# Token sums of the first half mixed and stored in the last block of the first phase, and two down splits ahead of the last products

## The chip, the cores and the metric

The kernel runs on one core of one Trainium2 chip. The metric is the device time of one execution in microseconds, the median of several runs; lower is better. The engines are TensorE (PE in the profile, its weight loads PEld), VectorE (DVE), ScalarE (ACT), GpSimd (POOL) and SyncE (SP). SP and POOL start the DMA transfers here, each through a queue of its own.

## What is computed

One layer of a hybrid encoder over 2048 tokens of width 1024, all in float32:

```
h = RMSNorm(x);  p = h @ W_in
A = sliding-window attention(p);  B = HGRN2 gated recurrence(p)
x = x + concat(A, B) @ W_out
h = RMSNorm(x);  gate, up = h @ W_gate_up
x = x + (silu(gate) * up) @ W_down          # 2816 hidden columns
```

Each float32 operand of a product is split into a high part (rounded for the fast matmul format) and a low part (the rest), and a product is three matmuls: high by high, low by high, high by low (`three_passes`, L201 to L211). ACT makes a high part by a copy, DVE makes the low part by a subtraction.

## The kernel before

There are two phases, each a block of its own in the program: all engines meet at its end.

**Phase A** (`build_phase_a`) takes 4 blocks of 512 tokens. In a block PE runs 16 chunks of weights: 12 of W_in (named KV, QA0, ... Q23, I23, G23) and 4 of W_out (WO0 to WO3), each in up to 4 groups of 128 tokens (or 2 heads) of about 3 us. The list `STEPS`, made by `block_steps`, says which smaller step follows which group: splits of the next chunk (`split_hi` on ACT, `split_lo` on DVE), attention steps, and recurrence steps such as `hb` and `hc` (gates), `ds` (the running state on DVE, L1015 and L1019), `att`, `o` (outputs, PE L833 and L838) and `on1` to `on3` (their norm). Every engine walks the same list in order and does its own part of each step; `left_out` or `of_next_block` skips steps in the last block. SP loads chunk n into one of two stages `a_w_stage` as soon as DVE has split chunk n-2 (L397). In WO0 to WO3 DVE adds each product to the residual (L919), ACT squares it (L571), and POOL stores it to the DRAM tensor `x_mid`. The projection results go through two banks `a_pj`, so a group needs the group two before it to have been read. In the last block SP loads the first 2 x 128 tokens to be mixed (L415) and the norm weights `n2w` (L417) into the stages, when the last splits have left them.

**Phase B** (`build_ffn`) forms the gate and up products by a scheme with 7 products (`P1`, `P6`, `P5`, `P2`, `P7`, `P3`, `P4`) in place of 8, on sums and differences of quarters of the weights and of the tokens. For the tokens, a half of 1024 tokens is 4 pairs of 128-token tiles. `mix` on DVE scales a pair by `rs` (the reciprocal root of its mean square, made by POOL) and `n2w` (2 instructions of 1024 columns), then makes 4 sums or differences of 512 columns; POOL stores three pieces of each pair into the DRAM tensor `hc`. When all 4 pairs are stored, POOL loads the seven operands `hx` from `hc` into two buffers; PE transposes each (`turn`, L1349), ACT and DVE split it (`h_high`, `h_low`). Before the first unit, DVE's order is: pair 0, the mix and the first split of the first weights, pairs 1 to 3, the second weight split, the first operand. Then 44 units (2 halves x 22 column tiles) run; the second half's pairs are mixed at units 4, 7, 10 and 13.

At the end 88 **down steps** multiply the stored activations by W_down. A step's operands are split by `high_down` on ACT and `low_down` on DVE. SP's order there is: the loads of steps 0 and 1, the store of the last unit's activations (`store_a`), the residual load (`load_res`, 2 MB), the loads of step 2 and on. DVE's order is: low parts of step 0, `up_halves`, `a_products` of the last unit, low parts of step 1.

## Time and profile before

| What | us |
|---|---|
| Median of 3 runs (2302.03 to 2303.75) | 2302.94 |
| The profiled execution, its own time | 2303.67 |
| Span of its trace | 2301.9 |
| PE busy in the span | 2199.6 (96%) |
| DVE busy | 1261.1 (55%) |
| ACT busy | 928.7 (40%) |
| POOL busy | 143.9 (6%) |
| Mean granted clock of PE | 0.984 of full speed |

Phase A runs from 0 to about 885 us, the first 44 units of phase B to about 1811 us, the down steps from there to the end.

How to read it: 96% busy says that PE is the engine that sets the time nearly everywhere. The page also cuts the span in 40 slices of 57.5 us with the busy tenths of each engine; PE has 9 in nearly all of them, and 3 and 6 in the two slices at the change of phase, where the granted clock is lower as well (7 tenths and 7 tenths of full speed as the mean of each slice).

### The profile page before, as it was taken

What the parts mean: (1) busy time and instruction counts of PE and PEld (TensorE: products, weight loads), DVE (VectorE), ACT (ScalarE), POOL (GpSimd) and SP (SyncE); (2) the same over time, 40 slices, a digit from 0 to 9 for tenths busy, and PEclk for the clock granted to TensorE, in tenths of its full rate; (3) what the DMA queues carried; (4) which work ended last, traced back from release to release, by engine and by line L of the source; (5) the groups of instructions that cost most, each with busy time, mean ns of one, the idle gap of its engine ahead of it and who ended that gap; (6) DMA issues with size and microseconds to landing.
All of it is one profiled execution on the core that took longest, in us unless ns stands there. A gap on an engine that the chain in (4) does not pass through costs nothing.

```text
span 2301.9 us, 31427 instructions
## 1 busy us (share of the span) xinstructions
PE 2199.6 (96%) x12640; PEld 1903.9 (83%) x12640; DVE 1261.1 (55%) x1902; ACT 928.7 (40%) x1674; POOL 143.9 (6%) x154
## 2 busy tenths in 40 slices
PE   7999999999999993699999999999999999999999
PEld 7889988998898893588888888888888788888887
DVE  4675466447635754556666566555555334343333
ACT  4773386448535741333333333333333222232222
POOL 2001201010112002100000000000000000000000
PEclk9999999999999997799999999999999999999999
DMA  3412332323133125623334233222221435445453
GB/s 133 146 58 102 119 112 74 129 92 112 56 138 119 56 93 189 240 84 133 133 133 151 83 137 119 83 82 83 83 83 65 150 139 187 178 180 186 172 193 134
DMA packets 81648, 284.00 MB, mean 123 GB/s; under 512 B 8608, under 2 KB 17056, under 8 KB 66912
## 3 DMA queue, kind: packets, MB, share of 16 engines
q1 hardware_dynamic: 67296, 221.96, 27.2%
q0 software_dynamic: 14208, 60.04, 7.1%
q8 instruction: 100, 1.64, 0.3%
q14 instruction: 44, 0.36, 0.0%
HBM read 227.44 MB, written 54.53 MB: 122 GB/s over the span
## 4 chain that ended last, share of the span: by engine, by line
PE 58%; DMA 2%; DVE 1%; issue 0%; DVEq 0%; POOL 0%; ACT 0%; SPq 0%; POOLq 0%
PE b_bank_A L209 3%; PE b_bank_A L208 3%; PE b_bank_C L209 3%; PE b_bank_B L209 3%; PE b_bank_B L208 3%; PE b_bank_B L210 3%; PE b_bank_A L210 3%; PE b_bank_C L208 3%; PE b_bank_C L210 3%; PE b_hx_bank L1400 3%; PE b_hx_bank L1402 3%; PE b_hx_bank L1401 3%; PE b_bank_D L208 2%; PE b_bank_D L209 2%; PE b_bank_D L210 2%; PE b_hx_bank L1349 1%
## 5 line engine op out<-in xcount | busy, mean ns | idle before, releaser
L1418 DVE TENSOR_TENSOR b_dn_lo<-b_dn_stage,b_dn_hi 128x1024 fp32r<-128x1024 f32 x88 | 107.8, 1226 | 303.8 <-ACT b_dn_hi L1302 303.7
L208 PE MATMUL a_pj<-a_w_hi,a_hT_hi 128*128 128x256 f32 x896 | 259.0, 289 | 1.7 <-issue 1.7
L209 PE MATMUL a_pj<-a_w_lo,a_hT_hi 128*128 128x256 f32 x896 | 253.3, 283 | 0.0
L210 PE MATMUL a_pj<-a_w_hi,a_hT_lo 128*128 128x256 f32 x896 | 253.3, 283 | 0.0
L1302 ACT ACTIVATE b_dn_hi<-b_dn_stage 128x1024 fp32r<-128x1024 f32 x88 | 93.3, 1060 | 341.8 <-PE b_bank_D L1402 310.6
L208 PEld LDWEIGHTS a_pj<-a_w_hi,a_hT_hi 128*128 128x128 f32 x896 | 171.6, 191 | 6.8 <-issue 4.4
L855 DVE TENSOR_TENSOR a_w_lo<-a_w_stage,a_w_hi 128x2048 fp32r<-128x2048 f32 (+1 forms) x64 | 137.9, 2155 | 71.2 <-ACT a_w_hi L518 71.2
L209 PEld LDWEIGHTS a_pj<-a_w_lo,a_hT_hi 128*128 128x128 f32 x896 | 171.7, 192 | 0.0
L210 PEld LDWEIGHTS a_pj<-a_w_hi,a_hT_lo 128*128 128x128 f32 x896 | 171.6, 191 | 0.0
L1400 PE MATMUL b_hx_bank<-b_dn_hi,b_a_hi 128*128 128x512 f32 x352 | 138.3, 393 | 4.9 <-DVE b_a_lo L1418 4.8
L1402 PE MATMUL b_hx_bank<-b_dn_hi,b_a_lo 128*128 128x512 f32 x352 | 137.9, 392 | 0.0
L1401 PE MATMUL b_hx_bank<-b_dn_lo,b_a_hi 128*128 128x512 f32 x352 | 137.9, 392 | 0.0
L208 PE MATMUL b_bank_A<-b_h_hi_B,b_w_hi 128*128 128x512 f32 x352 | 137.6, 391 | 0.0
L208 PE MATMUL b_bank_B<-b_h_hi_T,b_w_hi 128*128 128x512 f32 x352 | 137.3, 390 | 0.0
L209 PE MATMUL b_bank_A<-b_h_lo_B,b_w_hi 128*128 128x512 f32 x352 | 137.2, 390 | 0.0
L210 PE MATMUL b_bank_A<-b_h_hi_B,b_w_lo 128*128 128x512 f32 x352 | 137.0, 389 | 0.0
L210 PE MATMUL b_bank_B<-b_h_hi_T,b_w_lo 128*128 128x512 f32 x352 | 137.0, 389 | 0.0
L209 PE MATMUL b_bank_B<-b_h_lo_T,b_w_hi 128*128 128x512 f32 x352 | 136.9, 389 | 0.0
L1335 ACT ACTIVATE b_gate<-b_u 128x512 f32<-128x512 f32 x44 | 27.8, 632 | 241.3 <-DVE b_u L1541 241.3
L518 ACT ACTIVATE a_w_hi<-a_w_stage 128x2048 fp32r<-128x2048 f32 (+1 forms) x64 | 115.3, 1801 | 1.5 <-DMA a_w_stage<-w_whole 1.5
L1418 DVE TENSOR_TENSOR b_w_lo<-b_mixed_w,b_w_hi 128x1024 fp32r<-128x1024 f32 x88 | 107.6, 1222 | 11.5 <-ACT b_w_hi L1277 11.5
L1321 ACT ACTIVATE b_s<-b_bank_C 128x512 f32<-128x512 f32 x44 | 26.4, 600 | 206.3 <-PE b_bank_C L210 206.3
(266 smaller groups left out, 5557.6 us busy)
## 6 DMA issues: line engine op xcount, KB each, us to landing
a_w_stage<-w_whole SPq DMA_DIRECT2D x56, 1024.0 KB, 4.7
b_gu_stage<-w_gu SPq DMA_DIRECT2D x44, 1024.0 KB, 5.2
b_dn_stage<-w_dn SPq DMA_DIRECT2D x88, 512.0 KB, 3.4
a_mid<-b_a SPq DMA_DIRECT2D x88, 256.0 KB, 4.1
b_a_stage<-a_mid SPq DMA_DIRECT2D x88, 256.0 KB, 3.6
b_hx<-hc POOLq DMA_DIRECT2D x14, 1024.0 KB, 5.1
a_x_res<-x_pad POOLq DMA_DIRECT2D x16, 512.0 KB, 4.4
x_mid<-a_x_res POOLq DMA_DIRECT2D x16, 512.0 KB, 3.4
```

The costliest lines, as they stand in the source:

```text
L208: pe.matmul(out, stationary[0](k), moving[0](k), start=(k == 0 and not adds), stop=False, skip_group_check=adds)
L209: pe.matmul(out, stationary[0](k), moving[1](k), start=False, stop=False, skip_group_check=adds)
L210: last = pe.matmul(out, stationary[1](k), moving[0](k), start=False, stop=(k == ends), skip_group_check=adds)
L518: act.activation(w_hi[s][:, :, 0:cols], w_stage[s][:, :, 0:cols], ACT.Copy).then_inc(w_hi_ready.sem, 1)
L855: dve.tensor_tensor(w_lo[s][:, :, 0:cols], w_stage[s][:, :, 0:cols], w_hi[s][:, :, 0:cols].bitcast(F32), ALU.subtract).then_inc(w_lo_ready ...
L1302: act.activation(f.dn_hi[b][:], f.dn_stage[b][:], ACT.Copy).then_inc(f.dn_hi_ready, 1)
L1321: act.activation(f.s5[:], f.bank["C"][:], ACT.Copy).then_inc(f.s5_ready, 1)
L1335: act.activation(f.gate[1][:], f.u2[:], ACT.Silu).then_inc(f.silu_ready[1], 1)
L1400: pe.matmul(f.down[i], f.a_hi[b][:, rows], f.dn_hi[b][:, cols], start=(j == 0), stop=False)
L1401: pe.matmul(f.down[i], f.a_hi[b][:, rows], f.dn_lo[b][:, cols], start=False, stop=False)
L1402: last = pe.matmul(f.down[i], f.a_lo[b][:, rows], f.dn_hi[b][:, cols], start=False, stop=(j == FT - 1))
L1418: dve.tensor_tensor(out, full, hi.bitcast(F32), ALU.subtract).then_inc(ready, 1)
```

## The change

1. The mixing of the first half moves from the start of phase B into the last block of phase A, as eight steps `("mix", p, part)` in `STEPS`, on DVE. Part 0 is the two scalings, part 1 the four sums. They lie after Q23 group 1, I23 group 1, I23 group 3, G23 group 0, and in pairs after WO0 group 2 and WO1 group 3. Other blocks skip them (`left_out`).
2. There is one buffer, `a_mix_x` with `a_mix_t`, on the place that the block's input and Q/K had. SP loads each pair and, when DVE has mixed it, stores its three pieces (`store_mixed`); a load waits until the pair before it has landed in `hc`. These transfers stand between SP's loads of the weight chunks. `n2w` is loaded during the block; POOL makes the first eight `rs` at the step `vmix`.
3. When phase A ends, SP has also loaded the first unit's weights (`kept.gu_stage`) and the first operand (`kept.hx`), each after the split that leaves its stage. In phase B SP loads the second unit's weights and `n2w` at once, and POOL starts with operand 1.
4. In phase B the first operand's split goes ahead of the second weight split, on ACT and on DVE.
5. The split of down step 1 moves: `high_down(1)` right behind `high_down(0)`, and `low_down(1)` between `up_halves` and `a_products` of the last unit. SP's order there is as it was.

The numbers of the second half's mixing stay the same (one buffer then, as before).

```diff
@@ block_steps
+    after("Q23", 1, ("mix", 0, 0))
+    after("I23", 1, ("mix", 0, 1))
+    after("I23", 3, ("mix", 1, 0))
+    after("G23", 0, ("mix", 1, 1))
...
+    after("WO0", 2, ("mix", 2, 0), ("mix", 2, 1))
+    after("WO1", 3, ("mix", 3, 0), ("mix", 3, 1))
...
+def mix_tokens(dve, x, t, rs, at, n2w, mixed, part):
+    if part == 0:
+        for two in range(2):
+            last = dve.scalar_tensor_tensor(out=x[:, two, :], in0=x[:, two, :], scalar=rs[:, at + 4 * two:at + 4 * two + 1], in1=n2w[:], op0=ALU.mult, op1=ALU.mult)
+            if two == 0:
+                last.then_inc(mixed, 1)
+    else:
+        dve.drain()
+        dve.tensor_tensor(t[:, 0, :], x[:, 1, 0:512], x[:, 0, 0:512], ALU.subtract)
+        dve.drain()
+        dve.tensor_tensor(x[:, 1, 0:512], x[:, 1, 512:D], x[:, 1, 0:512], ALU.subtract).then_inc(mixed, 1)
+        dve.tensor_tensor(t[:, 1, :], x[:, 1, 512:D], t[:, 0, :], ALU.subtract)
+        dve.drain()
+        dve.tensor_tensor(t[:, 2, :], t[:, 1, :], x[:, 0, 512:D], ALU.subtract).then_inc(mixed, 1)
+def store_mixed(eng, hc, half, p, x, t, mixed, before, stored):
+    to = hc[half].rearrange("b r q c -> r q b c")[:, p]
+    eng.wait_ge(mixed, before + 1)
+    eng.dma_start(to[:, 0:2], x[:, 0, :].rearrange("r (b c) -> r b c", b=2)).then_inc(stored, 16)
+    eng.wait_ge(mixed, before + 2)
+    eng.dma_start(to[:, 2:4], x[:, 1, :].rearrange("r (b c) -> r b c", b=2)).then_inc(stored, 16)
+    eng.wait_ge(mixed, before + 3)
+    eng.dma_start(to[:, 4:7], t[:]).then_inc(stored, 16)
@@ build_phase_a, sync
+        def load_mix(p):
+            if p > 0:
+                sp.wait_ge(hc_stored, 48 * p)
+            sp.dma_start(mix_x[:], mid_pairs[0, p]).then_inc(mix_in, 16)
...
                 sp.wait_ge(w_lo_ready.sem, w_lo_ready.upto(b, max(n - 2, 0)))
                 load(n)
-
+                if b == NB - 1 and n == CHUNK_AT["Q23"]:
+                    sp.wait_ge(kT_full.sem, kT_full.upto(b, 1))
+                    load_mix(0)
+                    sp.wait_ge(sc_full.sem, sc_full.upto(b, 8))
+                    sp.dma_start(n2w[:], dram["n2w"]).then_inc(n2w_in, 16)
+                if b == NB - 1 and n in (CHUNK_AT["G23"], CHUNK_AT["WO0"] + 1):
+                    p = 0 if n == CHUNK_AT["G23"] else 1
+                    store_mixed(sp, hc, 0, p, mix_x, mix_t, mixed, 3 * p, hc_stored)
+                    load_mix(p + 1)
+
+        store_mixed(sp, hc, 0, 2, mix_x, mix_t, mixed, 6, hc_stored)
+        load_mix(3)
         sp.wait_ge(w_lo_ready.sem, w_lo_ready.upto(NB - 1, NW - 2))
-        sp.dma_start(kept.mix_x[:], x_mid.rearrange("(h two q p) d -> h q p two d", h=2, two=2, q=4, p=P)[0, 0]).then_inc(kept.mix_in, 16)
+        sp.dma_start(kept.gu_stage[:], dram["w_gu"][0]).then_inc(kept.gu_loaded, 16)
+        store_mixed(sp, hc, 0, 3, mix_x, mix_t, mixed, 9, hc_stored)
+        sp.wait_ge(hc_stored, 4 * 48)
         sp.wait_ge(w_lo_ready.sem, w_lo_ready.upto(NB - 1, NW - 1))
-        sp.dma_start(kept.n2w[:], dram["n2w"]).then_inc(kept.n2w_in, 16)
+        sp.dma_start(kept.hx[:], hc[0, HC.index(RIGHT[0])]).then_inc(kept.first_hx_loaded, 16)
@@ build_ffn, sync
-        load_weights(0)
-        sp.wait_ge(f.hc_stored[1], 2 * 48)
         load_weights(1)
+        sp.dma_start(f.n2w[:], dram["n2w"]).then_inc(f.n2w_in, 16)
@@ build_ffn, gpsimd
-        for p in range(PAIRS):
-            store_mix(0, p)
-            if p + 2 < PAIRS:
-                load_mix(0, p + 2)
-        for m in range(2):
-            pool.wait_ge(f.hc_stored[m], 2 * 48)
-        for q in range(NP):
-            load_hx(0, q)
+        for q in range(1, NP):
+            load_hx(0, q)
+            if q == 1:
...
@@ build_ffn, scalar
         w1_high(0)
+        h_high(0, 0)
         w2_high(0)
-        h_high(0, 0)
         h_high(0, 1)
...
             if unit == UNITS - 1:
                 high_down(0)
+                high_down(1)
...
-        for s in range(1, STEPS_DOWN):
+        for s in range(2, STEPS_DOWN):
@@ build_ffn, vector
-        dve.wait_ge(f.n2w_in, 16)
-        mix(0, 0)
         mix_weights(0)
         w1_low(0)
-        for p in range(1, PAIRS):
-            mix(0, p)
+        h_low(0, 0)
         w2_low(0)
-        h_low(0, 0)
         h_low(0, 1)
...
         low_down(0)
         up_halves(UNITS - 1)
+        low_down(1)
         a_products(UNITS - 1)
```

**SP in the last block and at the change of phase.** Before (`a_w_stage` are chunk loads, the first row here is that of WO2, `w_lo_ready` is DVE's split of the chunk two before; the rows after the branch belong to phase B):

```order
L399 DMA a_w_stage_51<-w_whole 128x2048 [waits w_lo_ready]
L399 DMA a_w_stage_52<-w_whole 128x2048 [waits w_lo_ready]
L415 DMA b_mix_x_53<-x_mid 128x2x1024 [waits w_lo_ready]
L417 DMA b_n2w<-n2w 128x1024 [waits w_lo_ready]
L1557 UNCONDITIONAL_BRANCH
L1168 UNCONDITIONAL_BRANCH [waits barrier_Pool_Activation_PE_DVE_SP_release]
L1173 DMA b_gu_stage_10620<-w_gu 128x2048
L1173 DMA b_gu_stage_10621<-w_gu 128x2048 [waits hc_stored1]
```

With the change, from the load of chunk Q23 to that of WO1:

```order
L444 DMA a_w_stage_52<-w_whole 128x2048 [waits w_lo_ready]
L458 DMA a_mix_x<-x_mid 128x2x1024 [waits kT_full]
L469 DMA a_n2w<-n2w 128x1024 [waits sc_full]
L444 DMA a_w_stage_51<-w_whole 128x2048 [waits w_lo_ready]
L444 DMA a_w_stage_52<-w_whole 128x2048 [waits w_lo_ready]
L236 DMA hc<-a_mix_x 128x2x512 [waits a_mixed]
L238 DMA hc<-a_mix_x 128x2x512 [waits a_mixed]
L240 DMA hc<-a_mix_t 128x3x512 [waits a_mixed]
L458 DMA a_mix_x<-x_mid 128x2x1024 [waits a_hc_stored]
L444 DMA a_w_stage_51<-w_whole 128x2048 [waits w_lo_ready]
L444 DMA a_w_stage_52<-w_whole 128x2048 [waits w_lo_ready]
```

The chunk loads of WO0 and WO1 (the last two rows) now stand behind the three stores of pair 0, which wait for DVE's mixing, and behind the load of pair 1, which waits until those stores have landed; before, nothing stood ahead of them but their own split.

**DVE in the last block, from the split of chunk G23 to the state of head 2** (`a_w_lo` is the split, `a_yH_lo` the step `yt 1`, `a_att_m` the step `att 2`, `a_f_gate` to `a_k_end` the step `hb 3`, `a_state` the step `ds 2`). Before:

```order
L855 TENSOR_TENSOR a_w_lo_72<-a_w_stage_52,a_w_hi_70 128x2048 [waits w_hi_ready]
L869 SCALAR_TENSOR_TENSOR a_yH_lo_98<-a_tr,a_gnw,a_yH_hi_96 128x512 [waits yH_hi_ready]
L1011 COPY_PREDICATED a_att_m<-a_causal,a_hb 128x512 [waits att_full]
L956 TENSOR_SCALAR a_f_gate_103<-a_f_gate_103 128x512 [waits lf_ready]
L958 SCALAR_TENSOR_TENSOR a_t_b<-a_not_start,a_t_a 128x512
L961 TENSOR_TENSOR a_t_a<-a_t_b 128x512
L966 TENSOR_TENSOR a_k_end_110<-a_t_b 128x512 [waits k_nat_ready]
L1015 COPY a_state<-a_carry 128x128 [waits tr_full]
L1019 SCALAR_TENSOR_TENSOR a_state<-a_state,a_decay,a_tr 128x128 x7
```

With the change, from the last sum of pair 0 on:

```order
L229 TENSOR_TENSOR a_mix_t<-a_mix_t,a_mix_x 128x512
L938 SCALAR_TENSOR_TENSOR a_yH_lo_102<-a_tr,a_gnw,a_yH_hi_100 128x512 [waits yH_hi_ready]
L1080 COPY_PREDICATED a_att_m<-a_causal,a_hb 128x512 [waits att_full]
L1025 TENSOR_SCALAR a_f_gate_107<-a_f_gate_107 128x512 [waits lf_ready]
L1027 SCALAR_TENSOR_TENSOR a_t_b<-a_not_start,a_t_a 128x512
L1030 TENSOR_TENSOR a_t_a<-a_t_b 128x512
L1035 TENSOR_TENSOR a_k_end_114<-a_t_b 128x512 [waits k_nat_ready]
L219 SCALAR_TENSOR_TENSOR a_mix_x<-a_mix_x,rs,a_n2w 128x1024 [waits a_mix_in]
L219 SCALAR_TENSOR_TENSOR a_mix_x<-a_mix_x,rs,a_n2w 128x1024
L1084 COPY a_state<-a_carry 128x128 [waits tr_full]
L1088 SCALAR_TENSOR_TENSOR a_state<-a_state,a_decay,a_tr 128x128 x7
```

Four sums of pair 0 (one shown) have come between the split and `yt 1`, and the two scalings of pair 1, which wait for that pair's load (`a_mix_in`), between `hb 3` and `ds 2`.

**DVE where the down steps begin** (`b_a` with `b_gate` is `a_products`, whose results `store_a` stores; `b_dn_lo` and `b_a_lo` are a down step's low parts). Before:

```order
L1489 TENSOR_TENSOR b_a_10630<-b_a_10630,b_gate_10628 128x512 [waits silu_ready0,up_half_ready]
L1489 TENSOR_TENSOR b_a_10631<-b_a_10631,b_gate_10629 128x512 [waits silu_ready1,up_half_ready]
L1418 TENSOR_TENSOR b_dn_lo_10638<-b_dn_stage_10640,b_dn_hi_10636 128x1024 [waits dn_hi_ready]
L1418 TENSOR_TENSOR b_a_lo_10644<-b_a_stage_10646,b_a_hi_10642 128x512 [waits al_hi_ready]
L1418 TENSOR_TENSOR b_dn_lo_10637<-b_dn_stage_10639,b_dn_hi_10635 128x1024 [waits dn_hi_ready]
```

With the change:

```order
L1521 TENSOR_TENSOR b_a_10716<-b_u_10712,b_s_10710 128x512 [waits a_stored1,s5_ready]
L1471 TENSOR_TENSOR b_dn_lo_10720<-b_dn_stage_10722,b_dn_hi_10718 128x1024 [waits dn_hi_ready]
L1471 TENSOR_TENSOR b_a_lo_10726<-b_a_stage_10728,b_a_hi_10724 128x512 [waits al_hi_ready]
L1527 TENSOR_TENSOR b_a_10715<-b_a_10715,b_gate_10713 128x512 [waits silu_ready0,up_half_ready]
L1527 TENSOR_TENSOR b_a_10716<-b_a_10716,b_gate_10714 128x512 [waits silu_ready1,up_half_ready]
L1471 TENSOR_TENSOR b_dn_lo_10719<-b_dn_stage_10721,b_dn_hi_10717 128x1024 [waits dn_hi_ready]
```

The two rows of down step 1 have moved ahead of the two products of the last unit.

## Rows read from the trace of the kernel before

**Rows 1.** Windows: length, busy PE, PEld, DVE, ACT, POOL, clock, DMA share, GB/s.
```profile
793.00:885.00 92.00, 89.47 (x749) 85.93 (x747) 45.80 (x78) 37.27 (x89) 7.09 (x8) 1.00 0.27 93
...
890.00:943.00 53.00, 0.05 (x1) 0.06 (x1) 27.51 (x32) 3.58 (x4) 15.59 (x20) 0.50 0.78 287
943.00:952.00 9.00, 8.33 (x36) 7.55 (x37) 3.67 (x3) 4.08 (x4) 1.06 (x2) 0.52 0.44 177
```

**Rows 2.** Waits of PE between 790 and 950 us: total, times, longest.
```profile
PE b_hx_bank L1349 <- DMA b_hx<-hc: 58.3, 1, 58.3
PE a_hb L833 <- DVE a_carry L1019: 0.7, 1, 0.7
```

**Rows 3.** Timeline, the change of phase: start, duration, engine, line, operation, [idle before].
```profile
890.90 0.71 POOL L1231 DMA_DIRECT2D b_mix_x<-x_mid  x1 [3.94 <-POOLq L1557]
...
890.47 0.33 SPq L1173 DMA_DIRECT2D b_gu_stage<-w_gu  x1
```

**Rows 4.** Timeline, one mixing and the first unit's preparation on DVE, ACT and PE.
```profile
893.56 2.48 DVE L1431 SCALAR_TENSOR_TENSOR b_mix_x<-b_mix_x,b_rs,b_n2w 128x1024 f32<-128x1024 f32 x2 [7.49 <-POOL b_rs L1253]
...
899.04 0.68 DVE L1448 TENSOR_TENSOR b_mixed_w<-b_gu_stage 128x512 f32<-128x512 f32 x1
...
901.78 0.68 DVE L1418 TENSOR_TENSOR b_w_lo<-b_gu_stage,b_w_hi 128x512 fp32r<-128x512 f32 x1
902.99 1.23 DVE L1418 TENSOR_TENSOR b_w_lo<-b_mixed_w,b_w_hi 128x1024 fp32r<-128x1024 f32 x1 [0.52 <-ACT b_w_hi L1277]
...
946.01 1.22 DVE L1418 TENSOR_TENSOR b_h_lo_B<-b_hx_bank,b_h_hi_B 128x1024 fp32r<-128x1024 f32 x1 [17.02 <-ACT b_h_hi_B L1291]
...
942.95 3.68 PE L1349 MATMUL b_hx_bank<-ident,b_hx 128*128 128x128 f32 x16 [58.33 <-DMA b_hx<-hc]
947.29 3.67 PE L1349 MATMUL b_hx_bank<-ident,b_hx 128*128 128x128 f32 x16 [0.67 <-DVE b_h_lo_B L1418]
```

**Rows 5.** DMA issues from 795 to 900 us: count, KB each, median us to landing.
```profile
a_w_stage<-w_whole SPq DMA_DIRECT2D x3, 1024.0 KB, 4.7
...
b_mix_x<-x_mid SPq DMA_DIRECT2D x1, 1024.0 KB, 5.2
...
b_mix_x<-x_mid POOLq DMA_DIRECT2D x1, 1024.0 KB, 7.0
...
hc<-b_mix_t POOLq DMA_DIRECT2D x1, 768.0 KB, 3.9
```

**Rows 6.** DMA issues from 700 to 960 us, the same columns.
```profile
hc<-b_mix_t POOLq DMA_DIRECT2D x4, 768.0 KB, 6.6
```

**Rows 7.** Timeline, DVE in the last block, and ACT at the split of chunk WO0.
```profile
809.17 2.29 DVE L855 TENSOR_TENSOR a_w_lo<-a_w_stage,a_w_hi 128x2048 fp32r<-128x2048 f32 x1 [0.75 <-ACT a_w_hi L518]
811.78 0.75 DVE L869 SCALAR_TENSOR_TENSOR a_yH_lo<-a_tr,a_gnw,a_yH_hi 128x512 fp32r<-128x512 f32 x1 [0.32 <-ACT a_yH_hi L661]
...
815.29 0.69 DVE L966 TENSOR_TENSOR a_k_end<-a_t_b 128x512 f32<-128x512 f32 x1
...
818.80 0.23 DVE L1015 COPY a_state<-a_carry 128x128 f32<-128x128 f32 x1 [2.82 <-PE a_tr L826]
...
820.08 1.91 ACT L518 ACTIVATE a_w_hi<-a_w_stage 128x2048 fp32r<-128x2048 f32 x1
```

**Rows 8.** Timeline, DVE in the output products of the last block.
```profile
850.10 0.42 DVE L919 TENSOR_TENSOR a_x_res<-a_x_res,a_pj 128x256 f32<-128x256 f32 x1 [2.46 <-PE a_pj L210]
```

**Rows 9.** Timeline, DVE and PE where the down products begin.
```profile
1813.34 1.22 DVE L1418 TENSOR_TENSOR b_dn_lo<-b_dn_stage,b_dn_hi 128x1024 fp32r<-128x1024 f32 x1
1814.48 0.68 DVE L1418 TENSOR_TENSOR b_a_lo<-b_a_stage,b_a_hi 128x512 fp32r<-128x512 f32 x1
...
1826.79 0.77 PE L1400 MATMUL b_hx_bank<-b_dn_hi,b_a_hi 128*128 128x512 f32 x1 [4.83 <-DVE b_a_lo L1418]
```

**Rows 10.** Busy time by stretch, columns of rows 1, after that wait.
```profile
1827.00:1832.00 5.00, 5.00 (x12) 3.89 (x13) 1.60 (x2) 0.26 (x1) 0.00 (x0) 0.50 0.85 306
1832.00:1840.00 8.00, 8.00 (x36) 6.62 (x35) 1.83 (x2) 1.58 (x2) 0.00 (x0) 0.98 0.13 38
```

More of the change, by code:

```diff
@@ L145, in of_next_block, with left_out @@
     return step[0] in ("sq", "n1a", "n1b", "xT") or step[0] in ("split_hi", "split_lo") and step[1] == NW
+def left_out(step, b):
+    return of_next_block(step) if b == NB - 1 else step[0] == "mix"
 LAST_YT_AT = 3
@@ L466, in _ @@
             for step in STEPS:
-                if of_next_block(step) and b == NB - 1:
+                if left_out(step, b):
                     continue
@@ L554, in _ @@
             for step in STEPS:
-                if of_next_block(step) and b == NB - 1:
+                if left_out(step, b):
                     continue
@@ L702, in _ @@
             for step in STEPS:
-                if of_next_block(step) and b == NB - 1:
+                if left_out(step, b):
                     continue
@@ L1040, in _ @@
                     mean_square_x(b)
+                elif kind == "mix":
+                    p, part = step[1:]
+                    if part == 0:
+                        if p == 0:
+                            dve.wait_ge(rs_ready, 1)
+                            dve.wait_ge(n2w_in, 16)
+                        dve.wait_ge(mix_in, 16 * (p + 1))
+                    mix_tokens(dve, mix_x, mix_t, kept.rs, p, n2w, mixed, part)
                 elif kind == "n1b":
```

129 lines of the change are left out of this document (55 added, 74 removed).

## The prediction

> **What bounds the kernel now.** I read the page's busy shares and its 40 slices first: PE is busy 96% of the span, so only the places where it isn't can give much. Two slices stand out, at the change of phase. The stretches around it [rows 1] show PE full until 885 us (89.47 of 92 us from 793 on), idle for the next 58 us, and DVE busy for half of that idle stretch (27.51 of 53 us). The reader is to see there also that the granted clock is 0.50, the lower of its two levels (1.2 against 2.4 GHz), until about 952 us. The waits of PE [rows 2] name the releaser: a single wait of 58.3 us for the transfer of the first operand from `hc`. Its largest wait for DVE in the last block is 0.7 us. So the boundary is bound by a chain that runs beside an idle PE (load a pair, mix it, store it, four times, then load the operand), and the last block of phase A is bound by PE with next to no slack against DVE.
>
> **Part 1: the boundary.** SP and POOL issue their first transfers of phase B at 890.47 and 890.90 [rows 3], some 5.5 us after PE's last product at 885. In between the last store to `x_mid` lands and the engines meet. The change leaves that, and I count from 890.47 as t = 0. Before, operand 0 is transposed from t = 52.48 and operand 1 from t = 56.82 [rows 4]; the first product follows operand 1 on PE. With the change operand 0 and the first weights are there at t = 0. DVE then needs, by the same rows' starts: mixing the weights 899.04 to 901.78 = 2.74; the first two low parts with ACT between them 901.78 to 902.99 = 1.21 and 1.23; the first half of operand 0, 1.22. With 0.1 to start, 6.5 us. PE's 16 transposes (3.68, half of them 2.0 before ACT starts) and ACT's copies fit in that. Operand 1 has another limit: POOL issues it at t = 0.43, beside SP's 1 MB of weights and 0.5 MB of `n2w`. The nearest row is the same situation before: a pair's 1 MB issued by POOL beside the first weights landed after 7.0 us [rows 5], so t = 7.4, which is later than 6.5 and decides. The transposes of operand 1 start at 7.4 where they started at 56.8: **-49.4 us**. Bounds: 6.5 us (-50.3) if the load is not the last, and 8.5 (-48.3) if the third transfer costs another microsecond. The second weight split now comes behind operand 0 on both engines, 2 x 1.2 us on DVE; PE has 3.7 us of transposes and 3 us of product ahead of its need for operand 1's low parts, so I cost it at nothing; without that cover it would be 2.4 us.
>
> **Part 2: what the last block pays.** A pair takes 893.56 to 899.04 = 5.5 us [rows 4], 2.5 for the two scalings (part 0) and 3.0 for the four sums (part 1); four pairs are 22 us of DVE in a block where DVE is half idle (45.80 of 92 us) [rows 1]. The sum of the work fits; its place does not. I follow the three engines from the rows of the last block [rows 7].
>
> Pair 0, part 0 falls into an idle stretch. Part 1 starts when the split of G23 (start 809.17, 2.2 us to the next start) is done, 811.4, and ends at 814.4. The steps from 811.78 to 815.98 (end of the `a_k_end` row), 4.2 us, so end at 818.6. SP can issue the third store at 814.4 too. It lands 3.9 us later [rows 5], at 818.3; only then is pair 1 loaded, and lands 5.2 us later, at 823.5. DVE has stood at that load since 818.6: **a new wait of 4.9 us**, in order, with the running state of head 2 behind it. Part 0 of pair 1 ends at 826.1, where the state began at 818.80: 7.3 us late. Behind the state and `hc 3` comes part 1 of pair 1, 3.0 more, so the split of WO0 and `on1 2` and `on2 2` behind it are 10.3 late. PE waits for the state with its `o 2` products (0.7 us already before, [rows 2]), for `hc 3` with `kt 3`, and for `on2 2` with `att 3`. PE had no wait at `att 3` before, so some slack; I give it half a microsecond, and PE is 9.8 us late from there. ACT stands as well, since the chunk WO0 is now issued behind pair 1's load at about 818.7 and needs to be there at 820.08 [rows 7]; at the latest it takes its own 4.7 us [rows 5] after the pair and lands by 828, its split on ACT (1.9) ends by 830; DVE comes to its own part of that split only at 835. It adds nothing.
>
> The Trainium skill, DMA: Bandwidth & Descriptors, "Anatomy of one DMA", says that a transfer's wait on a semaphore is spent on the issuing sequencer before dispatch, which speaks against putting these stores between SP's chunk loads. Its fit of 2.0 us plus bytes over 436 GB/s would give, as an estimate, 3.8 and 4.4 us for the store and the load, 0.9 us less wait than by the rows; the whole sum would be that much lower. No row of before shows SP storing to `hc`.
>
> PE would be idle for 8 us ahead of `o 2` (0.7 + 7.3). After an idle stretch of 4.83 us elsewhere [rows 9] the clock is at 0.50 for the next 5 us and back at 0.98 of full after it [rows 10]. At half speed the group G23 2 would take 6 us instead of 3 while PE is not what is waited for, so I take **+1.0** (0 to 3). In the output products the additions come 2.88 us apart (2.46 idle + 0.42) [rows 8], while a pair takes 5.5 us of DVE in one piece. Two banks cover one product; the addition after WO0 2 comes 5.9 us after the last one, so PE waits about half a microsecond, and again after WO1 3: **+1.1**. Pair 2 is mixed by 847.2 (850.10 - 2.88) + 10.8 + 0.4 + 5.5 = 863.9; pair 3's load is issued when its stores have landed, 3.9 later, and lands at 873.0, while DVE gets there four additions after 850.10, at 861.6 + 11.3 + 0.4 = 873.3: no wait, but no slack. Together phase A ends 9.8 + 1.0 + 1.1 = **11.9 us later**.
>
> Bounds: with 4.7 us for the load as for a chunk, no loss of clock and no later waits, 9.3. With the 6.6 us that the stores to `hc` take in the median over the busy stretch [rows 6] and 7.0 for the load it is 4.5 us more at pair 1 and as much at pair 3: with the clock's 3, about 22. I take the values of [rows 5] since the traffic in the last block (0.27 of the DMA engines) is that of their stretch.
>
> **Part 3: the first products of phase B.** PE worked 4.3 us on operand 1 and the first product until the clock rose at 952. Now its first transposes lie at t = 0, with a gap up to 7.4. Where it rises after the first product instead of in it, 2.7 us of matmuls take twice that: I take **+1.0** (0 to 3).
>
> **Part 4: the down steps.** PE waits 4.83 us [rows 9] for step 2's operands, whose loads stand on SP behind the last store and the 2 MB of residual. These in turn start when `a_products` is done. Moving the low parts of step 1 (1813.34 to 1815.16, 1.8 us) ahead of `a_products` makes SP's store, the residual and step 2's loads 1.8 us later. PE gains nothing: step 1 already ran right behind step 0. So **+1.8** (0 to 2).
>
> **The sum.** -49.4 + 11.9 + 1.0 + 1.8 = -34.7 us. The profiled execution took 2303.67 us (span 2301.9), 0.73 over the median; it becomes 2269.0, and so is forecast. The second half's mixing, the weights' loads and the other waits are as before: nothing.
>
> **The rivals.**
> 1. *The last block pays little* (10%): pair 1 lands before DVE gets to it, and the rest lies in DVE's idle time. For it: DVE is half idle there. Against it: load and store would have to take 4 us together where the rows give 8.6 at the least. By bounds of 3 us for phase A: 2303.7 - 49.4 + 3 + 1 + 1.8 = 2260.
> 2. *Both transfers are late* (20%): the stores land after 6.6 us, pairs 1 and 3 both make DVE stand: 2303.7 - 49.4 + 22 + 1 + 1.8 = 2279. For it: SP's queue then holds the store, a pair and two chunks. Against it: the transfers of [rows 5] had neighbours as well.
> 3. *Slower than before* (2%): the wait at `o 2` drops the clock, and the short waits behind it (`kt 3`, `att 3`, `o 3`) keep it at 1.2 GHz. PE has some 52 us of work left in phase A and, with the boundary's idle time between, could carry the low level into the first units. Each microsecond of work at full speed costs one more, so beyond 35 us of such work the gain is gone; 50 us in phase A and 10 behind it would give 2269 + 60 - 2 = 2327. Against it: in [rows 10] the clock was back within 6 us of dense matmuls. The Trainium skill, TensorE: Matmul & The Clock Gate, Part 1, has the clock return after a spell of sustained work, which that row agrees with.
> 4. *The boundary moves but something else holds operand 1* (1%), the time within 0.2% of before: it would need 35 us of new waits in all, and no row shows a candidate.
>
> The forecast has the other 67%.
>
> **How the numbers follow.** The forecast's own bounds are 2303.7 - 50.3 + 9.3 = 2263 (with nothing for the clock or the down steps) and, short of rival 2, about 2276. To leave out no more than 2 in 10 I take in rival 1 and most of rival 2: 2258 to 2281. A measurement of this kernel can tell about 0.2% (4.6 us) from no change. All but rivals 3 and 4 are over 0.2% faster: 0.97; the same 0.01; slower 0.02.
>
> **What would show it.** In the changed kernel's profile: PE's wait for the first operand is gone, and the first transposes start about 6 us after phase A's last product; operand 1's transposes start some 7.4 us after SP's first transfer of phase B. In the last block `a_state` waits behind `a_mix_x` for a DMA, 5 us, and PE's `o 2` products (L833's counterpart) wait 8 us for it, with a granted clock of 0.50 behind. PE's wait for down step 2 is 6.6 us. The prediction is wrong if that wait in the last block is under 3 us or over 12, if pair 3 makes DVE stand for more than 3 us, or if operand 1 lands more than 3 us away from t = 7.4.

## The result, and the profile after

The changed kernel takes **2267.7 us** (median of 4 runs, 2266.9 to 2268.2) against 2303.3 for the kernel before beside it (2302.0 to 2303.8): ratio 0.9848, 95% interval 0.9833 to 0.9862, so faster by 36 us. The forecast was 2269.0, in a range of 2258 to 2281. The profiled execution took 2267.58 us (span 2265.8), against 2303.67 before: 36.1 us less, where the sum said 34.7.

The waits of PE over the whole span (total, times, longest). The one wait of 58.3 us of [rows 2] is gone, and these four are now the longest behind the start of the kernel:

```profile
PE a_hb L902 <- DVE a_carry L1088: 9.9, 4, 7.7
PE b_hx_bank L1453 <- DVE b_a_lo L1471: 6.7, 2, 6.5
PE b_hx_bank L1402 <- PEq L1593: 5.9, 1, 5.9
PE b_hx_bank L1402 <- DMA b_hx<-hc: 5.0, 1, 5.0
```

The 7.7 of the first is the `o 2` wait of the last block, which the prediction had at 8.0 (the other three are smaller ones of the blocks before it, as [rows 2] has one of 0.7). The 6.5 of the second is the wait at down step 2, 4.8 before [rows 9]. The third is the meeting of the engines between the phases, the fourth is operand 1.

Windows of the changed kernel, in the columns of [rows 1]:

```profile
820.00:826.00 6.00, 1.94 (x17) 1.73 (x15) 2.73 (x4) 3.02 (x5) 0.00 (x0) 0.99 1.03 414
826.00:833.00 7.00, 3.32 (x24) 3.12 (x24) 5.88 (x14) 1.96 (x2) 0.00 (x0) 0.52 0.46 146
833.00:840.00 7.00, 5.53 (x56) 5.06 (x53) 5.66 (x9) 2.02 (x10) 1.01 (x1) 1.00 0.58 204
...
860.00:885.00 25.00, 24.23 (x200) 23.83 (x199) 14.77 (x20) 8.10 (x20) 3.10 (x5) 1.00 0.95 335
```

PE is busy for 5.3 of the 13 us from 820 on; that is the stretch in which the last block pays. The clock falls to 0.52 there from 826 on, as forecast. And in the output products (860 to 885) the DMA engines are now full, 0.95, where they were at 0.34 before. The prediction reckoned with the 0.27 of [rows 1] for the whole last block; over the same window (793 to 885) it is now 0.56.

DVE's timeline in the last block (start, duration, line, [idle before]), the counterpart of [rows 7] and [rows 8]:

```profile
803.59 2.47 DVE L219 SCALAR_TENSOR_TENSOR a_mix_x<-a_mix_x,rs,a_n2w 128x1024 f32<-128x1024 f32 x2
...
823.20 2.48 DVE L219 SCALAR_TENSOR_TENSOR a_mix_x<-a_mix_x,rs,a_n2w 128x1024 f32<-128x1024 f32 x2 [4.57 <-DMA a_mix_x<-x_mid]
825.59 0.22 DVE L1084 COPY a_state<-a_carry 128x128 f32<-128x128 f32 x1
...
838.44 0.69 DVE L1098 TENSOR_TENSOR a_y_nat<-a_hb,a_o_rs 128x512 f32<-128x512 f32 x1 [1.12 <-POOL a_o_rs L513]
...
894.94 0.42 DVE L988 TENSOR_TENSOR a_x_res<-a_x_res,a_pj 128x256 f32<-128x256 f32 x1 [2.46 <-PE a_pj L250]
```

Pair 0's scalings ran at 803.59 without a wait. Pair 1's scalings start at 823.20, after DVE has stood 4.57 us for the load (forecast: 823.5 and 4.9). The running state of head 2 follows at 825.59 (it was 818.80, [rows 7]), and the last addition comes at 894.94 where it came at 884.65: 10.3 us later.

SP's timeline shows why (start, duration of the issue): the third store of pair 0 at 814.53, pair 1's load only when that has landed, 3.85 us later, and the chunks WO0 and WO1 (2 MB) right behind it on the same queue:

```profile
814.53 0.36 SPq L240 DMA_DIRECT2D hc<-a_mix_t  x1
818.38 0.36 SPq L458 DMA_DIRECT2D a_mix_x<-x_mid  x1
818.79 0.93 SPq L444 DMA_DIRECT2D a_w_stage<-w_whole  x2
```

The timeline at the start of phase B. SP's first transfer (t = 0) is at 900.74; operand 1 is issued at 901.19, and its transposes start at 909.39, t = 8.65:

```profile
900.74 0.34 SPq L1241 DMA_DIRECT2D b_gu_stage<-w_gu  x1
...
900.78 3.65 PE L1402 MATMUL b_hx_bank<-ident,b_hx 128*128 128x128 f32 x16 [5.88 <-PEq L1593]
901.13 0.43 SPq L1269 DMA_DIRECT2D b_n2w<-n2w  x1
901.19 0.56 POOL L1303 DMA_DIRECT2D b_hx<-hc  x1 [3.94 <-POOLq L1593]
...
905.87 2.35 DVE L1471 TENSOR_TENSOR b_h_lo_B<-b_hx_bank,b_h_hi_B 128x1024 fp32r<-128x1024 f32 x2
...
909.39 3.65 PE L1402 MATMUL b_hx_bank<-ident,b_hx 128*128 128x128 f32 x16 [4.97 <-DMA b_hx<-hc]
```

DVE begins operand 0's first low part at 905.87, t = 5.13, so that PE could have gone on at t = 6.35; the load decides, as forecast, but it takes 8.1 us and not 7.0. Not only SP's two transfers run beside it: POOL issues operand 2 (1 MB) at 904.74, 3.6 us behind operand 1.

The down steps, the counterpart of [rows 9]. SP's row is the last store of `a_products`' results:

```profile
1777.13 0.92 SPq L1246 DMA_DIRECT2D a_mid<-b_a  x2
...
1790.98 0.77 PE L1453 MATMUL b_hx_bank<-b_dn_hi,b_a_hi 128*128 128x512 f32 x1 [6.47 <-DVE b_a_lo L1471]
```

### The profile page after: what moved, and what is told of

Read it like the earlier page. It is cut to its first block, busy times and chain, and to the rows that moved or that the text cites. A ratio compares the mean times of both kernels' runs of the same rounds, so it can differ in the third digit from the quotient of the medians.

```text
span 2265.8 us, 31421 instructions
## 1 busy us (share of the span) xinstructions
PE 2201.5 (97%) x12640; PEld 1905.6 (84%) x12640; DVE 1259.6 (56%) x1902; ACT 928.9 (41%) x1674; POOL 132.3 (6%) x138
## 4 chain that ended last, share of the span: by engine, by line
PE 58%; DMA 1%; DVE 1%; issue 0%; ACT 0%; SPq 0%; DVEq 0%; ACTq 0%; POOLq 0%
PE b_bank_A L248 4%; PE b_bank_A L250 4%; PE b_bank_A L249 4%; PE b_bank_C L248 4%; PE b_bank_C L250 4%; PE b_bank_B L250 4%; PE b_bank_B L248 4%; PE b_bank_B L249 4%; PE b_bank_C L249 4%; PE b_hx_bank L1453 3%; PE b_hx_bank L1454 3%; PE b_hx_bank L1455 3%; PE b_bank_D L248 2%; PE b_bank_D L249 2%; PE b_bank_D L250 2%; PE b_hx_bank L1402 1%
```

## The experiments

All ratios are to the kernel before, run on the same chip in the same sitting. Two kernels are set beside each other by their medians, and by their traces where the medians are nearer than about 2 us, for the changed kernel itself moved by 1.2 us between two sittings, and its ratio from 0.9848 to 0.9854 (below). The first four runs stand beside a kernel before that was 0.7 us faster than the one beside the change (2302.6 against 2303.3), so where a difference to the change is given for them, the one reckoned from the kernel before stands with it.

**The down split put back**

```
             if unit == UNITS - 1:
                 high_down(0)
-                high_down(1)
...
-        low_down(1)
         a_products(UNITS - 1)
```

> The changed kernel with the split of down step 1 back behind the last a_products. Theory (step 1's split ahead of a_products only delays SP's last store, the residual and step 2's loads): PE's wait for step 2's low part goes from 6.5 us back to 4.8, SP's last store comes 1.7 us sooner after the first down matmul, the time falls by 1.7 us to 2266.0, ratio to the kernel before 0.9839. Rival (step 2's loads are held by something else, or step 1 is then late itself): PE waits at step 1, or still 6.5 at step 2, and the time stays at 2267.7 or rises.

Measured: 2266.5 us (2265.1 to 2267.7), ratio 0.9843 (0.983 to 0.9857). By time alone that can't be told from the changed kernel: 1.2 us less, or 0.5 reckoned from the kernel before. The trace shows the wait as expected (PE's timeline), and, in the second fence, what PE still waits for behind it (total, times, longest):

```profile
1789.15 0.77 PE L1452 MATMUL b_hx_bank<-b_dn_hi,b_a_hi 128*128 128x512 f32 x1 [4.82 <-DVE b_a_lo L1470]
```

```profile
PE b_hx_bank L1452 <- DVE b_a_lo L1470: 1.3, 2, 1.0
```

The wait is 4.8 again instead of 6.5, so the order of the splits does set it. But this execution doesn't gain by it. From the first matmul of step 2 (1789.15) to the last addition (2262.18) it takes 473.03 us, where the change takes 471.07. So the last addition comes as late as in the change (2262.05). Two things eat the gain: waits for late operands at two later steps, 1.3 us against 0.2 in the change, and the clock, which is at 0.50 for 5.7 us behind step 2 against 4.3. What the wait is worth needs the next run.

**The down split alone, on the kernel before**

> The kernel before with nothing of the change but the down split of step 1 ahead of a_products. Theory: PE's wait for step 2 goes from 4.8 to 6.5 us, everything else is as before: 1.7 us more, ratio 1.0007. Rival (the split ahead gives something, or nothing): 1.0000 or less, the wait at 4.8.

Measured: 2304.0 us (11 runs, 2302.6 to 2305.4), ratio 1.0004 (0.9995 to 1.0013): 0.8 us more, an interval that holds both nothing and 1.7. The wait is there in full, 6.59 us. But in the profiled execution half of the 1.76 us comes back at once. Windows right behind the wait, first of the kernel before, then of this one (columns of [rows 1]; the third number from the end is the clock):

```profile
1829.79:1830.79 1.00, 1.00 (x4) 0.71 (x4) 0.00 (x0) 0.00 (x0) 0.00 (x0) 0.50 1.05 395
1830.79:1831.79 1.00, 1.00 (x4) 0.81 (x3) 0.00 (x0) 0.00 (x0) 0.00 (x0) 0.50 0.97 354
1831.79:1832.79 1.00, 1.00 (x5) 0.82 (x4) 0.00 (x0) 0.00 (x0) 0.00 (x0) 0.76 0.30 113
```

```profile
1829.81:1830.81 1.00, 1.00 (x4) 0.81 (x3) 0.00 (x0) 0.00 (x0) 0.00 (x0) 0.50 0.86 320
1830.81:1831.81 1.00, 1.00 (x5) 0.73 (x5) 0.00 (x0) 0.00 (x0) 0.00 (x0) 0.75 1.07 340
1831.81:1832.81 1.00, 1.00 (x6) 0.82 (x5) 0.00 (x0) 0.00 (x0) 0.00 (x0) 1.00 0.99 336
```

Before, step 2 begins at 1826.79 and the clock is back half way through the last of its windows, 5.5 us later. Here it begins at 1827.81 and the clock is back at 1831.3, after 3.5 us. Two microseconds less of matmuls at half speed are one microsecond saved. Between these two traces that adds up: from the first matmul of step 2 to the last addition of the kernel it is 471.31 us before (1826.79 to 2298.10) and 470.45 here (1827.81 to 2298.26), so the longer wait costs 1.76, 0.9 comes back, and 0.9 is left, beside a measured 0.8.

The longer wait is not what gave it back, though. The other kept traces, read in the same windows of 1 us, have the clock at 0.50 behind step 2 for very different times after waits of nearly one length. After 4.8 to 4.9 us of waiting it is 5.5 (before), 5.7 (down split put back) and 3.4 us (all together). After 6.4 to 6.8 us it is 3.5 here, 4.3 in the change, 3.2 in the change run once more, 5.5 with operand 1 alone and 6.1 with the chunk WO0 first. The window in which it comes back with operand 1 alone, where step 2 begins at 1791.59 after 6.56 us:

```profile
1796.59:1797.59 1.00, 1.00 (x5) 0.82 (x4) 0.00 (x0) 0.00 (x0) 0.00 (x0) 0.76 0.73 289
```

That is 5.5 us, as in the kernel before, behind a wait 1.7 us longer. So how much of a wait the clock gives back differs from execution to execution, by up to 1.5 us, and one pair of traces can't price it. What the down split costs stays open between nothing and its 1.76 us.

**A second buffer for a pair**

```
-    mix_x = put("a_mix_x", [P, 2, D], F32, at=arena)
+    mix_x = [put("a_mix_x0", [P, 2, D], F32, at=arena)]
...
+    mix_x.append(put("a_mix_x1", [P, 2, D], F32, at=mem.at + D * 4))
...
                     sp.dma_start(n2w[:], dram["n2w"]).then_inc(n2w_in, 16)
+                    load_mix(1)
```

It lies over `a_qT`, behind `n2w`, which is free by then. The stores count on one semaphore per buffer, and the sums of a pair wait until `mix_t` has been stored.

> The changed kernel with a second buffer for a pair's tokens, so that pair 1 is loaded right behind pair 0; the mixing steps stand where they stood. Theory (DVE stands for pair 1's load, 4.6 us, and everything behind it is late by it): DVE's wait is gone, the running state of head 2 is 2.3 us late against the kernel before instead of 6.8, PE's wait at the o 2 products falls from 7.7 to some 3.2 us, and the time by 4.5 us to 2263.2 (ratio 0.9827). Rival (the mixing work itself, 11 us of DVE ahead of PE's consumers, sets the delay, or the clock does): less than 1 us of gain, 2267.

Measured: 2263.1 us (2261.4 to 2266.4), ratio 0.9831 (0.9817 to 0.9844), 4.6 us less than the change (3.9 reckoned from the kernel before) where 4.5 were expected; its runs scatter by 5.0 us. DVE's timeline, then windows:

```profile
818.31 2.47 DVE L219 SCALAR_TENSOR_TENSOR a_mix_x<-a_mix_x,rs,a_n2w 128x1024 f32<-128x1024 f32 x2
820.70 0.22 DVE L1086 COPY a_state<-a_carry 128x128 f32<-128x128 f32 x1
```

```profile
820.00:826.00 6.00, 2.92 (x25) 2.63 (x25) 4.98 (x13) 2.57 (x4) 0.00 (x0) 1.00 1.03 408
826.00:833.00 7.00, 5.56 (x60) 4.99 (x58) 6.17 (x8) 4.09 (x12) 0.51 (x1) 1.00 0.96 336
```

No wait for a load, the state 4.9 us sooner, PE's wait at `o 2` 3.1 instead of 7.7. The last addition comes at 890.02, 4.9 us sooner. The theory holds: the wait for pair 1's load is nearly half of what the last block pays (10.3). The clock stays at 1.00 in both windows, where the change had 0.52 in the second. The last addition gains as much as the state does and no more, so the slow stretch had cost nothing on top. PE's waits show where it went: at `att 3` PE waits 2.5 us for DVE here and 1.5 in the change. The last block still pays 5.4 us against the kernel before (884.65), with no wait for a load in it.

**The chunk WO0 ahead of pair 0's stores**

```
-                if b == NB - 1 and n in (CHUNK_AT["G23"], CHUNK_AT["WO0"] + 1):
-                    p = 0 if n == CHUNK_AT["G23"] else 1
+                if b == NB - 1 and n in (CHUNK_AT["WO0"], CHUNK_AT["WO0"] + 1):
+                    p = 0 if n == CHUNK_AT["WO0"] else 1
```

> The changed kernel with SP loading the weight chunk WO0 ahead of pair 0's stores and pair 1's load instead of behind them. Theory (ACT's wait of 2.9 us for that chunk costs nothing, since DVE comes to its own part of the split 5 us later): that wait is gone, pair 1 lands when it did, and the time stays within 0.5 us of 2267.7. Rival (ACT's squares and copies behind the late split hold the o and y steps): 1 to 3 us less.

Measured: 2267.9 us (2266.1 to 2269.4), ratio 0.9848 (0.9834 to 0.9861). ACT's wait of 2.9 us for the chunk is gone from its waits, and the time has not moved: the prediction's "it adds nothing" holds. DVE's wait for pair 1 is 5.1 instead of 4.6 (the load takes 5.1 us instead of 4.8), so the load didn't land sooner. Phase B begins at 900.69, where the change has 900.74.

**Operand 1 alone on the queues**

```
+        sp.wait_ge(f.hx_loaded[1], 16)
         load_weights(1)
         sp.dma_start(f.n2w[:], dram["n2w"]).then_inc(f.n2w_in, 16)
```

> The changed kernel with SP's first two transfers of phase B (the second unit's weights, 1 MB, and n2w, 0.5 MB) held back until operand 1 has landed. Theory (operand 1's 8.1 us are three transfers that share the DMA engines; alone it takes 5.1 as the others do in the median): it lands 5.6 us after SP's first instruction, the first low part of operand 0 on DVE at 6.35 decides instead, PE's wait for the load is gone, and operand 1's transposes start 2.3 us sooner: 2265.4 (ratio 0.9836). Rival (the 8.1 us are the load's own, its issue from POOL or the strided read of hc): nothing gained; or the second unit's weights come late: slower.

Measured: 2268.8 us (2268.0 to 2269.6), ratio 0.9854 (0.984 to 0.9867): no gain. The first half of the expectation is right and the second is wrong. PE's timeline:

```profile
901.40 3.65 PE L1403 MATMUL b_hx_bank<-ident,b_hx 128*128 128x128 f32 x16 [5.88 <-PEq L1594]
...
907.76 3.67 PE L1403 MATMUL b_hx_bank<-ident,b_hx 128*128 128x128 f32 x16 [2.72 <-DVE b_h_lo_B L1472]
...
914.85 1.91 PE L1403 MATMUL b_hx_bank<-ident,b_hx 128*128 128x128 f32 x16
...
921.42 1.94 PE L1403 MATMUL b_hx_bank<-ident,b_hx 128*128 128x128 f32 x16 [1.91 <-DMA b_hx<-hc]
```

SP has no transfer at the start here, so t = 0 is taken as 901.37, where ACT begins with the first weights, 0.03 us ahead of PE. Operand 1's transposes start at t = 6.4, 2.3 sooner, held by DVE. The load itself takes 5.2 us, with only operand 2's load beside it for its last 1.7 us: so it was the company of SP's two transfers that made it 8.1. Operand 2's turn at t = 13.5 still has it (15.7 in the change). At operand 3 it is gone: PE waits 1.9 us for its load, which takes 9.5 us beside the held-back weights and `n2w`, and starts it at t = 20.05, where the change did at 20.2 without a wait. The gain was given back two operands later. The time is 1.1 us over the change's; the clock at down step 2, back only after 5.5 us (above), is part of that in the profiled execution.

**The old order of the first unit's splits**

```
         w1_high(0)
+        w2_high(0)
         h_high(0, 0)
-        w2_high(0)
```

(and the same on DVE).

> The changed kernel with the second weight split of the first unit ahead of operand 0 again, as the kernel before had it. Theory (the order costs nothing, since operand 1's load at 8.65 us decides): operand 0's first low part ends 2.4 us later on DVE, at 8.8 us, which is 0.15 behind that load, and the time stays within 0.5 us of 2267.7. Rival (in the change's order the low parts of operand 1 come behind the second weight split and hold the first products): up to 2.4 us faster.

Measured: 2268.8 us (2267.5 to 2270.7), ratio 0.9852 (0.9838 to 0.9865), the same. SP's first transfer is at 900.99 here, and operand 1 starts 8.67 us later, now held by DVE for 5.2 us instead of by its load. The two limits lie 0.02 us apart (8.65 in the change):

```profile
909.66 3.68 PE L1402 MATMUL b_hx_bank<-ident,b_hx 128*128 128x128 f32 x16 [5.19 <-DVE b_h_lo_B L1471]
```

**The changed kernel once more**

> The changed kernel itself once more, beside the runs that are compared with it: 2267.7 us within 1 us, ratio 0.9848.

Measured: 2268.9 us (2266.6 to 2271.1), ratio 0.9854 (0.9841 to 0.9868). It is the comparison for the three runs that follow.

**One buffer, mixing moved into DVE's idle time**

```
-    after("I23", 1, ("mix", 0, 1))
-    after("I23", 3, ("mix", 1, 0))
-    after("G23", 0, ("mix", 1, 1))
+    after("I23", 3, ("mix", 0, 1))
...
-    after("WO0", 2, ("mix", 2, 0), ("mix", 2, 1))
-    after("WO1", 3, ("mix", 3, 0), ("mix", 3, 1))
+    after("WO0", 2, ("mix", 1, 1))
+    after("WO1", 3, ("mix", 2, 0))
+    after("WO2", 0, ("mix", 2, 1))
+    after("WO3", 0, ("mix", 3, 0))
+    after("WO3", 1, ("mix", 3, 1))
```

(`mix 1 0` goes behind `on3 2` in G23 3; SP's stores move as the expectation says.)

> The changed kernel with its one buffer, and the eight mixing parts moved to where DVE waits for PE anyway: pair 0's sums behind hb 3, pair 1's scalings in G23 3, all others in halves behind single additions of the output products; SP's chunk loads WO0 and WO1 ahead of pair 0's stores, WO2 and WO3 ahead of pair 1's. Theory (neither the amount of DVE work nor the traffic costs the last block anything, only its place and the wait for the load): PE's wait at o 2 is back at 1 us, the last addition comes 1 us later than before the change instead of 10.3, but pair 3 is mixed only 5 us before the end, so its stores and operand 0's load reach 2 to 3 us into phase B, of which 1 to 2 show: 2260 (ratio 0.9813). Rival (the work or the traffic has a price wherever it stands): 2265 to 2268.

Measured: 2264.6 us (2261.2 to 2265.7), ratio 0.9834 (0.982 to 0.9847), 4 us less than the change beside it where 7 to 8 were expected. PE's wait at `o 2` is back at 1.1, so the moves work until the output products. There the transfers are late. SP's timeline, POOL's last store of phase A, and DVE at pair 3:

```profile
869.38 0.36 SPq L241 DMA_DIRECT2D hc<-a_mix_t  x1
875.18 0.36 SPq L459 DMA_DIRECT2D a_mix_x<-x_mid  x1
...
891.14 0.33 SPq L483 DMA_DIRECT2D b_hx<-hc  x1
899.31 0.34 SPq L1242 DMA_DIRECT2D b_gu_stage<-w_gu  x1
```

```profile
891.86 0.76 POOL L530 DMA_DIRECT2D x_mid<-a_x_res  x1 [16.24 <-ACT a_junk L641]
```

```profile
881.91 2.48 DVE L220 SCALAR_TENSOR_TENSOR a_mix_x<-a_mix_x,rs,a_n2w 128x1024 f32<-128x1024 f32 x2 [5.24 <-DMA a_mix_x<-x_mid]
```

Pair 2's last store takes 5.8 us and pair 3's load 6.7, 12.5 together, where pair 1's took 3.85 + 4.8 = 8.7 in the change. Beside pair 3's load a 512 KB store of POOL runs (6.9 us), and SP's first unit of weights (1 MB) right behind it. DVE stands for 5.2 us, PE waits 2.9 us for a late addition, and the last addition comes at 890.31. Operand 0's load is only issued at 891.14, and phase B starts at 899.31, 9.0 us after the last addition instead of 5.8.

What phase B waits for is the last store to `x_mid`. POOL issues it at 891.86, 0.7 us behind operand 0's load, and the two run side by side: the load takes 6.0 us, to 897.1, and the store 6.6, to 898.5, where it takes 3.4 in the change. In all twelve kept traces phase B begins 0.85 to 0.95 us after that store has landed. So the late operand cost its 3.2 us by what it did to another transfer. It all came of the chain store, load, mix, store, load, which has no cover left when it runs at the end.

**Two buffers, mixing in DVE's idle time**

```
-    after("I23", 1, ("mix", 0, 1))
-    after("I23", 3, ("mix", 1, 0))
-    after("G23", 0, ("mix", 1, 1))
+    after("I23", 3, ("mix", 0, 1))
...
+    after("WO0", 2, ("mix", 1, 0))
+    after("WO0", 3, ("mix", 1, 1))
+    after("WO1", 0, ("mix", 2, 0))
+    after("WO1", 2, ("mix", 2, 1))
+    after("WO2", 0, ("mix", 3, 0))
+    after("WO2", 2, ("mix", 3, 1))
```

> As the run before, with a second buffer for a pair's tokens, so that pairs 1 to 3 can be mixed one load earlier (pair 3 ends 11 us before the last addition). Theory: the last addition comes 0.5 us later than before the change, operand 0 is there at the start of phase B, and the boundary is as in the changed kernel: 2267.7 - 9.8 = 2257.9 (ratio 0.9805). Rival: as of the run before, 2265 to 2268.

Measured: 2257.3 us (2256.8 to 2258.4), ratio 0.9805 (0.9791 to 0.9818). DVE's timeline:

```profile
860.45 0.69 DVE L226 TENSOR_TENSOR a_mix_t<-a_mix_x 128x512 f32<-128x512 f32 x1 [1.16 <-DMA hc<-a_mix_t]
...
879.13 0.75 DVE L992 TENSOR_TENSOR a_x_res<-a_x_res,a_pj 128x256 f32<-128x256 f32 x2 [3.10 <-DMA a_x_res<-x_pad]
...
885.65 0.42 DVE L992 TENSOR_TENSOR a_x_res<-a_x_res,a_pj 128x256 f32<-128x256 f32 x1 [2.45 <-PE a_pj L252]
```

The last addition is 1.0 us later than before the change (884.65), not 10.3, with all four pairs mixed on the same engine in the same block. The work had next to no price; its places and the wait for a load had. The DMA engines' load shows even here: DVE waits 2.0 us for two stores of `mix_t`, 1.6 for pair 3 and 3.1 for a residual tile, but two banks of products cover most of it. Phase B begins 5.8 us after the last addition again.

**All together**

In phase B, besides the down split put back and `n2w` behind the second unit's weights:

```
+        sp.dma_start(kept.hx_1[:], hc[0, HC.index(RIGHT[1])]).then_inc(kept.first_hx_loaded, 16)
...
-            if q >= 2:
+            if q >= 2 and (half, q) != (0, 3):
...
-        w1_low(0)
-        h_low(0, 0)
-        w2_low(0)
-        h_low(0, 1)
+        w1_low(0, (0,))
+        h_low(0, 0)
+        w1_low(0, (1,))
+        h_low(0, 1)
+        w2_low(0)
```

> The run before, with the down split of step 1 back behind a_products, operand 1 also loaded at the end of phase A (into a buffer of its own), operand 3 issued without waiting for operand 1's transposes, n2w moved behind the second unit's weights, and in the first unit the halves of operand 0 split ahead of the mixed weights and operand 1 ahead of the second weights. Theory: 1.7 us from the down steps; the transposes of operand 1 start 4.6 us into phase B instead of 8.65, with nothing late behind them since operands 2 and 3 land by then: 4 us; together 2257.9 - 5.7 = 2252.2 (ratio 0.978). Rival (as in the run with operand 1 alone, what is gained at operand 1 is given back at a later operand): 2256.

Measured: 2253.3 us (2251.9 to 2255.4), ratio 0.9787 (0.9774 to 0.9801). PE's timeline:

```profile
892.45 3.30 PE L1412 MATMUL b_hx_bank<-ident,b_hx 128*128 128x128 f32 x16 [6.47 <-PEq L1605]
897.07 2.23 PE L1412 MATMUL b_hx_bank<-ident,b_hx_first 128*128 128x128 f32 x16 [1.33 <-DVE b_h_lo_B L1481]
901.91 1.91 PE L1412 MATMUL b_hx_bank<-ident,b_hx 128*128 128x128 f32 x16
...
911.57 1.94 PE L1412 MATMUL b_hx_bank<-ident,b_hx 128*128 128x128 f32 x16 [0.50 <-DMA b_hx<-hc]
```

Operand 1 starts at t = 4.6 and operand 2 at 9.5 (15.7 in the change). This time it is kept: operand 4 waits 0.5 us, no more. The measured 4.0 us over the run before are less than the 5.7 expected, while the spans of the two profiled executions differ by 6.8 (2256.6 and 2249.8); the runs of either scatter by 1.6 and 3.4 us, so the size of that gain stays open between the two. Its sign doesn't, nor its place: PE's turn of operand 4 comes 4.6 us sooner than in the run before (911.57 for 916.15). This profiled execution is the fastest of its four and has a mean clock of 0.998, the others 0.995 to 0.997, so the 6.8 may hold some luck with the clock. How the gain splits between the operands and the down split put back, no run shows. It beats the change by 15.6 us and the kernel before by 49.5.

## Why the prediction was right

Step by step, in the profiled execution, against its own time of before:

| step | predicted | measured | read from |
|---|---|---|---|
| boundary, to operand 1's transposes | -49.4 | -48.2 | t = 8.65 instead of 56.82 |
| last block | +11.9 | +10.3 | SP's first transfer at 900.74, was 890.47 |
| from operand 1 to the down steps | +1.0 | +0.4 | 37.9 us sooner at operand 1, 37.5 at the first down product |
| down steps | +1.8 | +1.4 | +1.65 at step 2, 0.25 back by the last addition |
| sum | -34.7 | -36.1 | 2303.67 to 2267.58 |

The sum is nearer than its terms: the boundary gave 1.2 us less than forecast, and the three prices together were 2.6 us lower. That they cancel in part is luck.

**Boundary.** Right that operand 1's load decides. The price was taken from two transfers side by side ([rows 5], 7.0), and here SP's two ran beside it from the start, and operand 2 from 904.74: 8.1 us, transposes at 8.65. The bound of 8.5 for "the third transfer costs another microsecond" was about the case that came; operand 2 was not in the sum at all. That the new order of splits costs nothing was right, and the run with the old order shows it was no gain either: there DVE holds operand 1 to 8.67.

**Last block.** The mechanism was right in its place, cause and followers: DVE stands for pair 1's load, PE for the state at `o 2` (7.7, forecast 8.0), and `on2 2` comes 9.7 us late (838.44 for 828.73; forecast 10.3). The run with a second buffer bears it out: 4.5 us foretold, 4.6 measured (3.9 reckoned from the kernel before, and 4.9 at the last addition in the traces). The load took 4.8 where [rows 5] gave 5.2, and the store 3.85 where they gave 3.9. That was partly luck, for the premise behind these values, DMA engines at 0.27 as in [rows 1], did not come: they were at 0.82 from 818.4 to 823.2. Pair 3 had 0.5 us of room (its load, issued at 865.50, took 5.6, and DVE came at 871.59), where the sum had 0.3. The Trainium skill, DMA: Bandwidth & Descriptors, "Anatomy of one DMA", has for these sizes by its fit, as an estimate, 4.4 and 3.8, for transfers that GpSimd issues, while these were SP's; the trace lies between that and the rows at the load, and agrees at the store. It agrees too that such a wait is spent on the issuing sequencer: pair 1's load and two chunks stood behind the store on SP.

**The term that failed** is "+1.0 (0 to 3)" for the clock in the last block. The clock did fall to 0.52 there; but of that stretch only 3.0 us were matmuls (829.68 to 832.7), 1.5 us more than at full speed, and PE waited for DVE again at `att 3`, 1.5 us, where the run with a second buffer, at full clock, has 2.5. The slow matmuls ended inside that wait. The prediction had that condition in its own words ("while PE is not what is waited for") and then priced it all the same. The other 0.6 us are smaller: DVE is 9.7 late at `on2 2` and not 10.3, and PE's slack behind it was 0.7 us and not 0.5, since the first output products' additions come at 852.57 for 843.56, 9.0 late. The output products came near to what was foretold: they are 1.3 us later at the last addition than at the first, forecast 1.1. One of the bounds has a slip: with its own terms, both transfers late and 3 for the clock give 22.9 us and not "about 22", so that rival 2 would stand at 2280, still within the range.

**From operand 1 to the down steps.** The clock behaved as the term says, at half the price. Before, it rose 4.3 us after operand 1's transposes began. Now PE's first transposes (900.78 to 904.4) run at 0.50, the clock is at 1.00 from 904.4 to 907.8, when PE does nothing, and it is back at 0.50 when operand 1 starts (windows of the changed kernel):

```profile
905.00:907.00 2.00, 0.00 (x0) 0.00 (x0) 2.00 (x2) 2.00 (x3) 0.32 (x1) 1.00 1.03 430
908.00:914.00 6.00, 4.61 (x19) 4.45 (x20) 3.71 (x4) 2.36 (x3) 0.55 (x1) 0.50 0.92 375
```

It rises 5.3 us after operand 1's start. A microsecond more at half speed is half a microsecond, and 0.4 is measured.

**Down steps.** The wait grew by 1.65 (forecast 1.8). In the profiled executions the clock came back 4.3 us after step 2 began instead of 5.5, which gave 0.6 back, and small waits behind took some of that. The traces above show that such a return differs from execution to execution, so the term was right in its mechanism, and how near its size is stays open.

**The rivals.** Rival 1 (the last block pays little) needed a load and a store in 4 us and fell; what it says of DVE's idle time is true all the same, once the steps stand in it and there is a second buffer (10.3 to 1.0 us). Rival 2 (both transfers late) did not come in the change, since pair 3's load had room, but in the run with one buffer and late pairs it did: 5.8 and 6.7 us. Rival 3's idle stretch came, its lasting low clock didn't. Rival 4 had no case.

Not tried: whether the DMA engines could be relieved in the output products, by loading the first unit's weights earlier or later, and which of its neighbours slows a load (below).
